# Residual kept by token: back projections in eight banks, norms and boundaries by chunk of tokens, an unrolled program

## What is computed

```python
for i in range(DEPTH):
    h = rms_norm(x, mix_pre_g[i])
    m = ssd_mixer(h, ...) if i % 2 == 0 else shortconv_mixer(h, ...)
    x = x + rms_norm(m, mix_post_g[i])
    f = conv_ffn(rms_norm(x, ffn_pre_g[i]), ...)
    x = x + rms_norm(f, ffn_post_g[i])
```

## Time and profile before

| what | value |
|---|---|
| runs | 1438.22, 1438.89, 1440.73 us |
| span of the profiled execution, first to last instruction | 1436.1 us |
| what lies around the span (median less span) | 2.8 us |
| PE, busy share of the span | 97% |
| DVE, ACT, POOL | 57%, 40%, 9% |
| mean granted TensorE clock | 0.988 of full speed |

### The profile page before, as it was taken

The page is one execution under the profiler, slowest core; times in us unless marked ns, Lnnn a source line. Parts: engine busy times, 40 slices in busy tenths (PEclk is TensorE's granted clock), DMA queues, the critical chain, the costliest instruction groups (busy, mean ns, idle before and its releaser), DMA issues.

```text
span 1436.1 us, 18916 instructions
## 1 busy us (share of the span) xinstructions
PE 1400.2 (97%) x6549; PEld 1149.7 (80%) x6549; DVE 812.7 (57%) x1051; ACT 576.1 (40%) x790; POOL 135.7 (9%) x101
## 2 busy tenths in 40 slices
PE   8999999999999999999999989999999999999997
PEld 6788888888887788888888868888778888888886
DVE  4788888888425765656512275553376655652223
ACT  6666655556323433333422242223344333332222
POOL 0000000000113200000001050001240000000002
PEclk9999999999999999999999999999989999999999
DMA  4433233332232233333333313333313333333331
GB/s 130 132 111 99 82 102 102 102 117 78 84 88 74 59 102 98 92 102 89 98 95 91 95 44 90 101 98 93 88 44 103 91 99 102 88 99 90 101 90 60
DMA packets 243699, 133.02 MB, mean 93 GB/s; under 512 B 5629, under 2 KB 242101, under 8 KB 242645
## 3 DMA queue, kind: packets, MB, share of 16 engines
q1 hardware_dynamic: 243621, 132.54, 31.6%
q10 hardware_dynamic: 48, 0.07, 0.0%
HBM read 130.43 MB, written 2.16 MB: 92 GB/s over the span
## 4 chain that ended last, share of the span: by engine, by line
PE 86%; DVE 6%; ACT 5%; issue 2%; SPq 1%; DMA 0%; ACTq 0%; DVEq 0%
PE bank L1011 26%; PE bank L1010 26%; PE bank L1009 26%; DVE h_lo L880 2%; DVE xs L872 2%; PE bank L1205 1%; ACT mask L523 1%; PE bank L1213 1%; PE bank L1195 1%; ACT L510 1%; PE bank L1178 1%; ACT w_hi L418 1%; ACT feat L510 1%; ACT pad L504 1%; DVE side L864 1%
## 5 line engine op out<-in xcount | busy, mean ns | idle before, releaser
L1009 PE MATMUL bank<-h_hi,w_hi 128*128 128x512 f32 x1232 | 483.0, 392 | 0.1
L1011 PE MATMUL bank<-h_lo,w_hi 128*128 128x512 f32 x1232 | 479.7, 389 | 0.0
L1010 PE MATMUL bank<-h_hi,w_lo 128*128 128x512 f32 x1232 | 479.6, 389 | 0.0
L678 DVE TENSOR_TENSOR w_lo<-w_raw,w_hi 128x1024 fp32r<-128x1024 f32 (+2 forms) x235 | 287.4, 1223 | 302.6 <-ACT w_hi L418 302.6
L418 ACT ACTIVATE w_hi<-w_raw 128x1024 fp32r<-128x1024 f32 (+1 forms) x232 | 241.2, 1040 | 371.5 <-PE bank L1011 361.8
L1011 PEld LDWEIGHTS bank<-h_lo,w_hi 128*128 128x128 f32 x1232 | 231.3, 188 | 48.4
L1010 PEld LDWEIGHTS bank<-h_hi,w_lo 128*128 128x128 f32 x1232 | 231.5, 188 | 47.2
L1009 PEld LDWEIGHTS bank<-h_hi,w_hi 128*128 128x128 f32 x1232 | 231.4, 188 | 46.9 <-DVE w_lo L678 0.5
L370 POOL TENSOR_TENSOR total<-total,square 128x512 f32<-128x512 f32 x43 | 61.0, 1419 | 1201.2 <-ACT square L437 1201.2
L1011 PE MATMUL bank<-hid_lo,w_hi 128*128 128x512 f32 x416 | 165.9, 399 | 0.0
L1010 PE MATMUL bank<-hid_hi,w_lo 128*128 128x512 f32 x416 | 163.9, 394 | 0.0
(11 more groups left out here) (158 smaller groups left out, 1289.6 us busy)
## 6 DMA issues: line engine op xcount, KB each, us to landing
w_raw<-in_ffn_w_up SPq DMA_DIRECT2D x88, 512.0 KB, 3.8
w_raw<-in_ssd_w_in SPq DMA_DIRECT2D x48, 512.0 KB, 3.9
w_raw<-in_ffn_w_down SPq DMA_DIRECT2D x32, 512.0 KB, 3.8
w_raw<-in_sc_w_in SPq DMA_DIRECT2D x24, 512.0 KB, 3.7
acs_b<-acs_dram SPq DMA_DIRECT2D x8, 1024.0 KB, 6.3
w_raw<-in_ssd_w_out SPq DMA_DIRECT2D x16, 512.0 KB, 3.8
w_raw<-in_ffn_w_down SPq DMA_DIRECT2D x16, 384.0 KB, 3.3
w_raw<-in_sc_w_out SPq DMA_DIRECT2D x8, 512.0 KB, 3.8
```

Of the source, the lines that this page charges most:

```text
L678: return nc.vector.tensor_tensor(w_lo[:, slot, k0:kt, :], w_raw[:, slot, k0:kt, :], w_hi[:, slot, k0:kt, :].bitcast(F32), ALU.subtract)
L1009: nc.tensor.matmul(dst, wh, xh, start=start, stop=False)
L1010: nc.tensor.matmul(dst, wl, xh, start=False, stop=False)
L1011: return nc.tensor.matmul(dst, wh, xl, start=False, stop=stop)
```

## The change

- The residual is x_tok, tokens on partitions, in place from first load to last store. xs, m, turn_x, the final transposes and copies go.
- A back projection (`project`) keeps 128x128 tiles of the activations (hid_hi, hid_lo, y_hi, y_lo) in the array and streams rows of the weight: unit k is the whole row block k of the weight (a flat load, 1024 output features), and its two halves of 512 columns go to the two banks of each of four token chunks, so the result stands in all eight banks. The k tiles come in groups of 1, but for the first group (3 or 2) and the last (4); in the last group chunk after chunk is finished.
- The weight slots are three during SSD and five after it; loads and splits follow one list of units.
- A boundary goes by chunk: ACT squares a bank with the sum along the row (`post_sum`), DVE multiplies the bank by the gain row (`scale`) and adds to x_tok (`residual`), PE turns the chunk's eight tiles (`turn`), ACT and DVE read h_hi and h_lo out of the bank, 128 columns at a time (`high`, `low`), ACT sums x's squares (`pre_sum`). POOL does nothing there.
- The next projection begins with three units in two halves of 256 tokens each (`enter`, `half_unit`): the half of chunks 0 and 1 of all three units, then that of chunks 2 and 3. `two_units` and the keep_warm calls at boundaries go.
- The SSD norm of y is no longer applied to the rows: its sum of squares enters the root of the norm behind it (`q_tok`).
- The start loads the small parameters in another order, and makes the mask of the first SSD group behind the second convolution. The SSD groups are otherwise as before.
- There are no loops: every engine's program is written out in full.

The core of the diff, with what the prediction speaks of:

```diff
+    SLOTS = 5
+    def slot(u):
+        return u % 3 if u < U_OUT else (u - U_OUT) % SLOTS
...
+    LAST = 4
+    back = [
+        Back(0, U_OUT, [3] + [1] * (IT - 3 - LAST) + [LAST], [(6, 7), (0, 1), (2, 3), (4, 5)], IT, mix_post_g[0], (FFN_PRE, 0)),
+        Back(1, U_DOWN[0], [2] + [1] * (FT - 2 - LAST) + [LAST], [(2, 3), (4, 5), (6, 7), (0, 1)], FT, ffn_post_g[0], (MIX_PRE, 1)),
+        Back(2, U_SCO, [2] + [1] * (WT - 2 - LAST) + [LAST], [(0, 1), (2, 3), (4, 5), (6, 7)], WT, mix_post_g[1], (FFN_PRE, 1)),
+        Back(3, U_DOWN[1], [2] + [1] * (FT - 2 - LAST) + [LAST], [(4, 5), (6, 7), (0, 1), (2, 3)], FT, ffn_post_g[1], None),
+    ]
...
-                pool.wait_ge(m_done, norms // 2 * DT)
-                pool.wait_ge(row_done, norms)
-                for k in range(HERE if norms < 8 else HERE_LAST, DT):
-                    pool.tensor_tensor(m[:, k, :], m[:, k, :], r_post[:], ALU.mult).then_inc(upper_scaled, 1)
...
+                for u in range(split_at[0], min(end, U_END)):
+                    act.wait_ge(raw_landed[u % 2], 16 * (u // 2 + 1))
+                    if before(u) is not None:
+                        act.wait_ge(unit_done, before(u) + 1)
+                    elif u == U_OUT + 3:
+                        act.wait_ge(seg_done, GROUPS)
+                    elif u == U_OUT + 4:
+                        act.wait_ge(scan_done, GROUPS)
+                    nc.scalar.activation(w_hi[slot(u)][:], w_raw[:, u % 2, :], ACT.Copy).then_inc(w_hi_done, 1)
+                    split_at[0] = u + 1
...
-                with turns(act, 0, DT // 2, {xd: 2}) as i:
-                    for n in range(2):
-                        k = 2 * i + n
-                        act.wait_ge(x_done, xd.up())
-                        nc.scalar.activation(h_hi[:, bass.ds(k, 1), :], xs[:, bass.ds(k, 1), :], ACT.Copy,
-                                             scale=one(col_gain(*pre, k))).then_inc(h_hi_done, 1)
-                        nc.scalar.activation(squares[:, bass.ds(k, 1), :], xs[:, bass.ds(k, 1), :], ACT.Square).then_inc(squared, 1)
...
+            def post_sum(b, c, half):
+                if 2 * c + half < 7:
+                    act.wait_ge(proj_done, 7 * b.nth + 2 * c + half + 1)
+                else:
+                    act.wait_ge(unit_done, b.end)
+                at = 2 * c + half
+                if x_sums_so_far[0]:
+                    act.wait_ge(x_sq_done, x_sums_so_far[0])
+                nc.scalar.activation(r_row[:, half, :], bank[b.banks[c][half]][:], ACT.Square,
+                                     accum_out=sums[:, b.nth, at:at + 1]).then_inc(sq_done, 1)
+                act.wait_ge(sq_done, 8 * b.nth + at + 1)
+                if half == 0:
+                    if b.nth == 0 and c == 0:
+                        act.wait_ge(q_done, 1)
+                    nc.scalar.activation(rest_sum[:, b.nth, c:c + 1], sums[:, b.nth, at:at + 1], ACT.Identity,
+                                         bias=q_tok[:, c:c + 1] if b.nth == 0 else eps[:], scale=1.0 / D).then_inc(rest_done, 1)
+                else:
+                    act.wait_ge(rest_done, C * b.nth + c + 1)
+                    nc.scalar.activation(root[:, b.nth, c:c + 1], sums[:, b.nth, at:at + 1], ACT.Sqrt,
+                                         bias=rest_sum[:, b.nth, c:c + 1], scale=1.0 / D).then_inc(root_done, 1)
+            def pre_sum(b, c):
+                act.wait_ge(x_done, 8 * b.nth + 2 * c + 2)
+                if x_sums_so_far[0]:
+                    act.wait_ge(x_sq_done, x_sums_so_far[0])
+                x_sums_so_far[0] += 1
+                nc.scalar.activation(r_row[:].rearrange("p a t -> p (a t)"), x_tok[:, c, :], ACT.Square,
+                                     accum_out=x_sums[:, b.nth, c:c + 1]).then_inc(x_sq_done, 1)
+            def high(b, c):
+                for q in range(2):
+                    act.wait_ge(x_turned, 8 * b.nth + 2 * c + q + 1)
+                    for i in range(4):
+                        k = 4 * q + i
+                        last = nc.scalar.activation(h_hi[:, k, c * P:(c + 1) * P], bank[b.banks[c][q]][:, i * P:(i + 1) * P],
+                                                    ACT.Copy, scale=one(col_gain(*b.pre, k)))
+                    last.then_inc(hi_done, 1)
+            def boundary(b, first):
+                splits_to(b.end + 1)
+                post_sum(b, 0, 0)
+                post_sum(b, 0, 1)
+                if b.pre:
+                    pre_sum(b, 0)
+                post_sum(b, 1, 0)
+                post_sum(b, 1, 1)
+                if b.pre:
+                    high(b, 0)
+                    pre_sum(b, 1)
+                post_sum(b, 2, 0)
+                post_sum(b, 2, 1)
+                if b.pre:
+                    high(b, 1)
+                post_sum(b, 3, 0)
+                splits_to(b.end + AHEAD)
+                post_sum(b, 3, 1)
+                if not b.pre:
+                    return
+                high(b, 2)
+                pre_sum(b, 2)
+                pre_sum(b, 3)
+                high(b, 3)
+                act.wait_ge(x_sq_done, C * (b.nth + 1))
+                nc.scalar.activation(r_pre_tok[:, b.nth, :], x_sums[:, b.nth, :], ACT.Sqrt, bias=eps[:], scale=1.0 / D).then_inc(pre_root, 1)
+                splits_to(b.end + AHEAD + 1)
+                act.wait_ge(row_mm, b.nth + 1)
+                nc.scalar.copy(r_row[:, 0, :], bank[b.banks[3][0]][:]).then_inc(row_done, 1)
...
-            def scale(k, row):
-                nc.vector.tensor_tensor(side[:, k % 2, :], m[:, k, :], row, ALU.mult).then_inc(scaled_done, 1)
...
-                nc.vector.scalar_tensor_tensor(out=xs[:, k, :], in0=side[:, k % 2, :] if k < here else m[:, k, :],
-                                               scalar=one(col_gain(which, layer, k)), in1=xs[:, k, :],
-                                               op0=ALU.mult, op1=ALU.add).then_inc(x_done, 1)
...
+            def scale(b, c, half):
+                at = 8 * b.nth + 2 * c + half
+                cols = slice(half * HALF_D, (half + 1) * HALF_D)
+                if c == 0 and half == 0:
+                    dve.wait_ge(g_landed, 16 * (b.nth + 1))
+                dve.wait_ge(sq_done, at + 1)
+                nc.vector.tensor_tensor(scaled[:, c % 2, cols], bank[b.banks[c][half]][:], g_row[:, cols], ALU.mult).then_inc(scaled_done, 1)
+            def residual(b, c):
+                dve.wait_ge(root_done, C * b.nth + c + 1)
+                nc.vector.reciprocal(r_post[:, b.nth, c:c + 1], root[:, b.nth, c:c + 1]).then_inc(r_post_done, 1)
+                dve.wait_ge(scaled_done, 8 * b.nth + 2 * c + 2)
+                dve.wait_ge(r_post_done, C * b.nth + c + 1)
+                for half in range(2):
+                    cols = slice(half * HALF_D, (half + 1) * HALF_D)
+                    nc.vector.scalar_tensor_tensor(out=x_tok[:, c, cols], in0=scaled[:, c % 2, cols], scalar=r_post[:, b.nth, c:c + 1],
+                                                   in1=x_tok[:, c, cols], op0=ALU.mult, op1=ALU.add).then_inc(x_done, 1)
+            def low(b, c):
+                for q in range(2):
+                    dve.wait_ge(hi_done, 8 * b.nth + 2 * c + q + 1)
+                    for i in range(4):
+                        k, cols = 4 * q + i, slice(c * P, (c + 1) * P)
+                        last = nc.vector.scalar_tensor_tensor(out=h_lo[:, k, cols], in0=bank[b.banks[c][q]][:, i * P:(i + 1) * P],
+                                                              scalar=one(col_gain(*b.pre, k)), in1=h_hi[:, k, cols].bitcast(F32),
+                                                              op0=ALU.mult, op1=ALU.subtract)
+                    last.then_inc(lo_done, 1)
+            def boundary(b):
+                splits_to(b.end + 1)
+                scale(b, 0, 0)
+                scale(b, 0, 1)
+                residual(b, 0)
+                scale(b, 1, 0)
+                scale(b, 1, 1)
+                residual(b, 1)
+                if b.pre:
+                    low(b, 0)
+                scale(b, 2, 0)
+                scale(b, 2, 1)
+                residual(b, 2)
+                if b.pre:
+                    low(b, 1)
+                scale(b, 3, 0)
+                splits_to(b.end + 1 + 1)
+                scale(b, 3, 1)
+                residual(b, 3)
+                if not b.pre:
+                    return
+                splits_to(b.end + AHEAD)
+                low(b, 2)
+                low(b, 3)
+                dve.wait_ge(pre_root, b.nth + 1)
+                nc.vector.reciprocal(r_pre_tok[:, b.nth, :], r_pre_tok[:, b.nth, :]).then_inc(pre_done, 1)
+                splits_to(b.end + AHEAD + 1)
+                dve.wait_ge(row_done, b.nth + 1)
...
-            def norm_sum(tiles, spare=3):
-                pe.wait_ge(summed, sm.up(tiles))
-                for c in range(C):
-                    nc.tensor.matmul(bank[6][:, c:c + 1], total[:, c * P:(c + 1) * P], ones[:, 0:1], start=c == 0, stop=False)
```

(65 more changed lines are left out.)

1268 lines of the change are left out of this document (495 added, 773 removed).

## The result

Before 1438.86 us, after 1405.73 us (medians of four runs each, 1438.22 to 1440.73 and 1405.03 to 1406.38); ratio 0.9766, 95% interval 0.9754 to 0.9777. The profiled span fell by 32.8 us, from 1436.1 to 1403.3.

A forecast was written before the change was run, and what follows sets the result against it. PE bounds the kernel at its own pace, except at three inner boundaries (64.1 us) and the end (21.5). Terms -36.8 - 14.0 - 10.9 + 10.8 - 1.0 = -51.9 take the 1436.1 span to 1384.2, plus 2.8 gives 1387.0; range 1370 to 1412.

The forecast's parts named there:

- Step 1: Three inner boundaries: chunk work just covered by PE's matmuls, overhead 9.1 us each against 21.4, 21.5, 21.2; 36.8 us saved.
- my row: Line 1213, 128 columns loaded and 128 float32 streamed in 0.1275 us, taken as the half units' 256-column matmul time.
- Step 2: Behind the last matmul: 3.4 us of norm and adds plus 4.06 of store, 7.5 against 21.5; 14.0 us saved.
- Step 3: Back projections: 1632 matmuls stream w_hi and w_lo instead of y and hid, issuing at 0.2267 not 0.2333; 10.9 us saved.
- pace unchanged: Rival: back projections' pace does not change by what streams; 10.9 us more, 1398; chance 0.13.
- Step 4: Move to out projection: PE waits 7.8 us for unit 50's split behind y tiles, plus 3 for low clock; 10.8 lost.
- Step 5: Start: second unit 5 to 6 us earlier, but PE waits some 6 us for the silu; 1 saved.
- Step 6: SSD groups, among items put at nothing: PE sets their pace, so 0 us change.
- half units at 0.2267: Rival at boundaries: 256-column matmuls bound by weight load, 0.2267 us each; 43 us more, 1430; chance 0.10.
- A late chunk chain: Rival at boundaries: DVE and ACT late, each turn waits, 8 us a boundary; 24 more, 1411; chance 0.17.
- Instruction supply: Rival: fetching the written-out program stops PE 1.7 us a time; 31 stops eat the gain, 33 give 1443; chance 0.06.

The follow-up runs named there:

- high256: Changed kernel plus pads of 192, 224 and 224 bytes, so upper weight slots, hidden and y tiles start at 128 over a multiple of 256: 1388.87 us.
- out_split: Changed kernel with unit 50's split on ScalarE and VectorE right behind unit 49's, ahead of the y tiles, in the last head group: 1396.02 us.
- enter_whole: Changed kernel with each of the first three units behind a boundary running its two halves in succession, not all first halves first: 1422.81 us.
- The run with all changes: Changed kernel plus high256's pads, out_split, the third try's group order, an earlier fifth-unit split and reordered first-group ScalarE work: 1356.68 us.
- the second try: Changed kernel with third-unit splits moved earlier in the SSD groups and VectorE's fourth-unit split ahead of the second feature's taps: 1405.33 us.
- last1: Changed kernel with the last group of each back projection one tile instead of four (LAST = 1): 1438.50 us.
- two sound fixes: Changed kernel with third-unit splits earlier in SSD groups, 1405.89 us; then also VectorE's fourth-unit split earlier, 1405.33 us.
- the third: The second try plus a one-column Exp on ScalarE ahead of the second feature's eviction in groups 2 to 8: 1395.73 us.

## Why the prediction was right, and where it was wrong

The forecast was 1387, range 1370 to 1412; measured 1405.7, 18.7 us above the forecast and in the range. The sign, the place of the gain and the new stall were right. That the time still fell in the range is in part luck: steps 3, 5 and 6 came out 31 us worse than forecast, and steps 1, 2 and 4 gave 12 us of it back. By its steps, on the span:

| step | predicted | measured | by |
|---|---|---|---|
| 1 inner boundaries | -36.8 | -45.5 | table of stretches, pace and stall taken out |
| 2 the end | -14.0 | -15.8 | 5.7 against 21.5 us |
| 3 what streams | -10.9 | +7.1 | 6.1 in slots 3 and 4, 1.0 in the back projections |
| 4 stall | +10.8 | +9.1 | 7.58 of wait, 1.6 at low clock |
| 5 start | -1.0 | +1.1 | 12.4 less 11.3 |
| 6 SSD groups | 0 | +11.3 | 7 waits of 1.61 us |
| sum | -51.9 | -32.7 | the span fell by 32.8 |

**Step 1** was right in mechanism: the chunks stay ahead of PE, no turn waits, and the tail of chunk 3 ends under the half units. The overhead is 6 us a boundary rather than 9.1. Working for the first: 246.13 less 44 units at 0.2267 (239.4) leaves 6.7, plus 2.4 of turns ahead of it, less the 2.5 of pace that high256 took back there, 6.6. (The second gives 5.4 and the third 6.6; 64.1 less 18.6 is 45.5.) Terms that were too high: the 256-column matmul at 0.119 us, not 0.1275; the fifth unit at 1.31, 0.47 and 1.45, not 2; the turns at 0.79, not 0.87. The Trainium skill (TensorE: Matmul & The Clock Gate, LDWEIGHTS) has a load of 128 columns at 107 ns; 0.119 lies between that and my row, and the fastest half units, at 0.1133, are still above it. The run with LAST = 1 shows that the chunks stay ahead because of the last group of four. My row of 128 columns was of float32 and came near by chance: float32 matmuls of 256 columns (line 992) issue every 0.215 us at full clock (112 to 114 us).

**Step 2**: 1.8 us better. The last addition ends at 1400.8, 3.2 us behind the last matmul (3.4 forecast), and the store behind it took 2.5 us and not 4.06.

**Step 3** is the one that failed worst, by 18.0 us. Its observation was right (0.2333 for y and hid, 0.2267 for h) and so was the guess that placement sets the pace. But I took "a multiple of 64 bytes" from two cases and asked it of the streaming tile alone. What the runs show is a relation of both operands: the same remainder modulo 256. The stationary y and hidden tiles stand at 160 and 224 and w at 128 or 192, so the back projections gained nothing, and the new slots 3 and 4, at 192, made 41 whole units that stream h slower, by 24 x 0.0067 us each, 6.6 us; the four that run in halves there went somewhat faster, and high256 took 6.1 back. The other 1.0 is what the back projections took beyond turns and stall, half of it their pace, 0.2338 instead of 0.2333 in the down projections. With equal remainders the 10.9 us came as forecast (high256). My rival "pace unchanged" had the right sign of the correction, and its 10.9 us cover more than half of the 18.0.

**Step 4** was right by row and cause; the run out_split took 9.7 us back. The low clock cost 1.6 us where I took 3. The Trainium skill (same page, Part 1) says that a long idle brings the half clock, and the trace agrees: 0.50 at 379 to 381, and 0.59 at 484 to 487 in enter_whole.

**Step 5**: PE's wait for the silu is 6.39 us at 55.26, "some 6" as forecast, with the low clock behind it that I had called possible, so the turns removed there gave nothing. The run with all changes puts the silus first in that group, and its start is 6.6 us shorter.

**Step 6** failed by 11.3 us. "SSD groups: PE sets their pace" was read off the old trace; I did not follow the moved split. In the kernel before, VectorE's split stood at 122.13, ahead of the mask at 123.89; the change puts it behind, and in the code written out the table load stands on ScalarE's chain. That ScalarE's chain alone is enough for 11 us the second try shows; that VectorE's alone would be is inferred. That writing out is what moved the load is my reading too: no run has the old loop with the rest of the change. The slack in the old groups was never worked out, and that is the missing step.

The rivals: half units at 0.2267 are refuted by 0.119. A late chunk chain did not occur, and last1 shows its price, 32.8 us. Instruction supply: 51 and 21 fetch packets in place of 20 and 10, and no gap without a releaser is spread over PE's timeline. What the program written out cost was more likely in another place, the table load.

## What to carry to other kernels

Work on a boundary goes under matmuls if the result is finished in parts (four chunks behind a group of four k tiles, 33 us here) and if the next stage has something to do that needs only the first parts (first halves of three units, 17 us). When the order of an in-order queue changes, list for each queue what now stands ahead of what PE waits for, table loads included, and look for the wait that is second to last: here two sound fixes measured nothing before the third brought 10 us. Compare the start addresses of both operands of 512-column matmuls: pads of under 256 bytes gave 16.9 us here, and 10.0 in the kernel before.
